# Last stage of a fused layer kernel: inputs loaded during the stage before, and one of its products issued ahead

## The reference

```python
x = layer_norm(ALPHA * x + m, lp['ln1_g'], lp['ln1_b'])            # h below
x = layer_norm(ALPHA * x + grouped_moe(x, router_w, router_b, lp['e_w1'], lp['e_w3'], lp['e_w2']),
               lp['ln2_g'], lp['ln2_b'])
...
def layer_norm(x, g, b):
    mu = xf.mean(-1, keepdims=True)
    var = jnp.square(xf - mu).mean(-1, keepdims=True)
    return ((xf - mu) * lax.rsqrt(var + LN_EPS) * g + b)
...
gate = gate / gate.sum(-1, keepdims=True)     # two experts for each frame, in grouped_moe
out = out.at[tok_pad].add(y_pad * gate_pad)   # each frame: the sum of its two gated expert rows
```

## Time and profile before

| what | value |
|---|---|
| median of 3 runs | 3728.18 us (3726.44 to 3731.19) |
| profiled execution, its own time | 3730.97 us |
| its span in the trace | 3728.8 us |
| last record of PE in `experts` starts | 3609.45 us |
| `combine` starts (its first transfer is issued) | 3614.01 us |
| `combine`, to the end of the span | 114.8 us |

### The profile page before, as it was taken

How to read it: one execution, slowest core, us unless ns; L and a number is a source line. 1 busy time by engine, 2 the same in 40 slices (tenths; PEclk the granted TensorE clock), 3 DMA queues, 4 the chain that set the end, 5 groups by cost and what they waited for, 6 DMA issues and landing times. The chain is left out here.

```text
span 3728.8 us, 77062 instructions
## 1 busy us (share of the span) xinstructions
PE 3563.9 (96%) x30285; PEld 2173.9 (58%) x30286; DVE 1623.6 (44%) x3569; ACT 965.2 (26%) x1799; POOL 230.0 (6%) x350
## 2 busy tenths in 40 slices
PE   9999979999999999979999999969999999999988
PEld 5555559989898988845555655543333333333333
DVE  1222226676767777657777435541111111111118
ACT  3333322323232333235555401110000000000003
POOL 0000010000000000011100000000000000000005
PEclk9999989999999999979999999979999999999999
DMA  6222230000000000021011522236667576643437
GB/s 229 78 89 86 70 86 8 15 15 19 11 19 11 19 11 19 7 87 50 17 52 58 187 99 96 87 155 259 247 236 279 208 282 266 256 184 136 165 120 300
DMA packets 146576, 430.57 MB, mean 115 GB/s; under 512 B 30712, under 2 KB 78976, under 8 KB 134016
## 3 DMA queue, kind: packets, MB, share of 16 engines
q1 hardware_dynamic: 127776, 359.27, 26.2%
q0 software_dynamic: 11616, 42.21, 3.2%
q10 hardware_dynamic: 6912, 25.17, 1.8%
HBM read 750.99 MB, written 78.27 MB: 222 GB/s over the span
## 5 line engine op out<-in xcount | busy, mean ns | idle before, releaser
L791 PE MATMUL rp_pa<-r_xT,w_rwkv 128*128 128x128 f32 x3808 | 480.4, 281 | 10.9 <-DMA r_xT<-scratch_xT 10.9
L307 PE MATMUL fp<-f_w,f_xT 128*128 128x411 f32 (+1 forms) x1360 | 483.0, 511 | 2.2 <-ACT f_xT L374 2.2
L791 PEld LDWEIGHTS rp_pa<-r_xT,w_rwkv 128*128 128x128 f32 x3808 | 446.6, 193 | 37.8 <-issue 26.7
L307 PEld LDWEIGHTS fp<-f_w,f_xT 128*128 128x128 f32 x1360 | 253.4, 190 | 199.3 <-issue 196.4
L2934 PE MATMUL e_H<-rows_in,e_xT 128*64 128x512 f32 x768 | 347.1, 606 | 19.1 <-DMA rows_in<-in_moe_w 17.4
L2935 PE MATMUL e_H<-fy,e_xT 128*64 x768 | 346.9, 606 | 0.0
L2953 PE MATMUL e_Y<-e_w,e_gT 128*64 128x512 f32 x768 | 339.8, 595 | 1.0 <-DMA e_w<-in_moe_w 1.0
L2935 PE MATMUL e_H<-e_w,e_xT 128*64 x768 | 339.8, 595 | 0.0
L2954 PE MATMUL e_Y<-e_w,e_gT 128*64 x768 | 339.8, 595 | 0.0
L2934 PE MATMUL e_H<-shared,e_xT 128*64 128x512 f32 x768 | 339.8, 595 | 0.0
L2934 PEld LDWEIGHTS e_H<-rows_in,e_xT 128*64 128x64 f32 x768 | 107.0, 140 | 239.0 <-issue 215.0
(11 more groups left out here) (440 smaller groups left out, 5590.9 us busy)
## 6 DMA issues: line engine op xcount, KB each, us to landing
e_w<-in_moe_w SPq DMA_DIRECT2D x144, 2048.0 KB
fy<-in_moe_w SPq DMA_DIRECT2D x48, 2048.0 KB
rows_in<-in_moe_w SPq DMA_DIRECT2D x48, 2048.0 KB
shared<-in_moe_w SPq DMA_DIRECT2D x48, 2048.0 KB
scratch_ypad<-e_y ACTq DMA_DIRECT2D x48, 512.0 KB, 2.7
scratch_xT<-f_xT SPq DMA_DIRECT2D x17, 512.0 KB, 5.3
r_xT<-scratch_xT SPq DMA_DIRECT2D x17, 512.0 KB, 3.8
scratch_h<-m_h SPq DMA_DIRECT2D x17, 512.0 KB, 2.6
```

Of the source, the lines that this page charges most:

```text
L307: mm = eng.matmul(A[n][:, 0:width], xT[:, t % 2, k, :], w[:, k, CUTS[n]:CUTS[n + 1]], start=(k == 0), stop=(k == KD - 1))
L791: mm = eng.matmul(pre_bank(bank)[:, f * P:(f + 1) * P], w[:, d, (i + f) * P:(i + f + 1) * P], xT[:, slot, d, :], start=(d == 0), stop=(d = ...
```

## The change

- After its last weight load in `experts`, SP issues the loads of all 17 tiles' frames and of the two parameter rows, 19 transfers of 512 KB, into `shared[0]` (tiles 0 to 3), `fy` (4 to 11), `rows_in` slot 1 (12, 13), `e_x` (14, 15) and `shared[1]` (16); `gain` and `offset` go to `rows_in` slot 0. In front of the parameter rows there is a wait for "h1" of block 47, in front of the last load one for "h3" of block 47.
- `combine` lies inside the scope that holds these places, and has no frame loads of its own. On SP only the 17 stores are left.
- PE makes the frame products of both halves of a tile together. Those of tiles 0 to 3 come first; that of tile t + 2 comes behind the y products of tile t, from t = 2 on.

```diff
--- before.py
+++ after.py
@@ -2889,6 +2889,20 @@
             body(BLOCKS - 2, 0)
             body(BLOCKS - 1, 1, last=True)
 
+
+            def frames(t):
+                sp.dma_start(keep["z_h"][t], io["h"][t * P:(t + 1) * P, :]).then_inc(keep["z_h_loaded"][t % 4], 16)
+
+            for t in range(4):
+                frames(t)
+            sp.wait_ge(*pe.after("h1", BLOCKS - 1))
+            sp.dma_start(keep["z_gain"], io["ln2_g"].broadcast_to([P, D])).then_inc(keep["z_weights_loaded"], 16)
+            sp.dma_start(keep["z_offset"], io["ln2_b"].broadcast_to([P, D])).then_inc(keep["z_weights_loaded"], 16)
+            for t in range(4, NT):
+                frames(t)
+            sp.wait_ge(*pe.after("h3", BLOCKS - 1))
+            frames(NT)
+
         @block.gpsimd
         def _(eng):
             pool.begin(eng)
@@ -3063,16 +3077,15 @@
 
         SLOTS = 4
         Z = [ctx.enter_context(nc.psum_tensor(f"z_Z{s}", [P, D], F32)) for s in range(SLOTS)]
-        gain, offset = sb("z_gain", [P, D]), sb("z_offset", [P, D])
-        h = sb("z_h", [P, SLOTS, D])
+        gain, offset, h = keep["z_gain"], keep["z_offset"], keep["z_h"]
         y = sb("z_y", [P, SLOTS, 2, D])
         scaled = sb("z_scaled", [P, P])
         diag = sb("z_diag", [P, SLOTS, 2, P])
         z = sb("z_z", [P, SLOTS, D])
         stats, mv, std = sb("z_stats", [P, SLOTS, 2, 6]), sb("z_mv", [P, SLOTS, 5]), sb("z_std", [P, SLOTS])
-        weights_loaded = sem("z_weights_loaded")
+        weights_loaded = keep["z_weights_loaded"]
         scaled_made = sem("z_scaled_made")
-        h_loaded = [sem(f"z_h_loaded{s}") for s in range(SLOTS)]
+        h_loaded = keep["z_h_loaded"]
         y_loaded = [sem(f"z_y_loaded{s}") for s in range(SLOTS)]
         stored = [sem(f"z_stored{s}") for s in range(SLOTS)]
         pe = Steps(sem("z_pe_steps"), ["sum"])
@@ -3089,12 +3102,6 @@
 
         @block.sync
         def _(sp):
-            def load(t):
-                s, _ = turn(t)
-                if t >= SLOTS:
-                    sp.wait_ge(*pe.after("sum", t - SLOTS))
-                sp.dma_start(h[:, s, :], io["h"][t * P:(t + 1) * P, :]).then_inc(h_loaded[s], 16)
-
             def store(t):
                 s, _ = turn(t)
                 sp.wait_ge(*pool.after("out", t))
@@ -3102,15 +3109,7 @@
                 dst = io["y_sample"][0] if t == NT else io["y_prompt"][0, t * P:(t + 1) * P, :]
                 sp.dma_start(dst, z[0:NEW if t == NT else P, s, :]).then_inc(stored[s], 16)
 
-            load(0)
-            load(1)
-            sp.dma_start(gain[:, :], io["ln2_g"].broadcast_to([P, D])).then_inc(weights_loaded, 16)
-            sp.dma_start(offset[:, :], io["ln2_b"].broadcast_to([P, D])).then_inc(weights_loaded, 16)
-            load(2)
-            load(3)
             for t in range(TILES):
-                if t + SLOTS < TILES:
-                    load(t + SLOTS)
                 store(t)
             for s in range(SLOTS):
                 sp.wait_ge(stored[s], 16 * len(range(s, TILES, SLOTS)))
@@ -3143,20 +3142,33 @@
         def _(eng):
             pe.begin(eng)
             eng.wait_ge(scaled_made, 1)
-            for t in range(TILES):
+
+            def frame(t):
                 s, n = turn(t)
-                eng.wait_ge(h_loaded[s], 16 * (n + 1))
+                eng.wait_ge(h_loaded[s], 16 * len(range(s, TILES, SLOTS)))
                 if t >= SLOTS:
                     eng.wait_ge(*act.after("norm", t - SLOTS))
                 for half in (0, 1):
                     at = slice(half * HALF, (half + 1) * HALF)
-                    eng.matmul(Z[s][:, at], scaled[:, :], h[:, s, at], start=True, stop=False)
-                    if half == 0:
-                        eng.wait_ge(*diags.after("diag", t))
-                        eng.wait_ge(y_loaded[s], 32 * (n + 1))
+                    eng.matmul(Z[s][:, at], scaled[:, :], h[t][:, at], start=True, stop=False)
+
+            def experts_rows(t):
+                s, n = turn(t)
+                eng.wait_ge(*diags.after("diag", t))
+                eng.wait_ge(y_loaded[s], 32 * (n + 1))
+                for half in (0, 1):
+                    at = slice(half * HALF, (half + 1) * HALF)
                     for i in (0, 1):
                         mm = eng.matmul(Z[s][:, at], diag[:, s, i, :], y[:, s, i, at], start=False, stop=(i == 1))
                 mm.then_inc(*pe.done("sum"))
+
+
+            for t in range(SLOTS):
+                frame(t)
+            for t in range(TILES):
+                experts_rows(t)
+                if SLOTS <= t + 2 < TILES:
+                    frame(t + 2)
 
         @block.scalar
         def _(eng):
@@ -3264,9 +3276,18 @@
                                       for n in ("w1", "w3", "w2")}
             keep["e_second_loaded"] = {n: inner.enter_context(nc.semaphore(f"e_{n}_second_loaded"))
                                        for n in ("w1", "w3", "w2")}
+
+            spots = [keep["shared"][0][:, t, :] for t in range(4)]
+            spots += [keep["fy"][:, 2 * t:2 * t + 2, :].rearrange("p a b -> p (a b)") for t in range(NT // 2)]
+            spots += [keep["rows_in"][:, 1, 0:D], keep["rows_in"][:, 1, D:2 * D]]
+            spots += [keep["e_x"][:, 0, :], keep["e_x"][:, 1, :], keep["shared"][1][:, 0, :]]
+            keep["z_h"] = spots
+            keep["z_gain"], keep["z_offset"] = keep["rows_in"][:, 0, 0:D], keep["rows_in"][:, 0, D:2 * D]
+            keep["z_weights_loaded"] = inner.enter_context(nc.semaphore("z_weights_loaded"))
+            keep["z_h_loaded"] = [inner.enter_context(nc.semaphore(f"z_h_loaded{p}")) for p in range(4)]
             mix(nc, io, keep)
             experts(nc, io, keep)
-        combine(nc, io, keep)
+            combine(nc, io, keep)
 
 
 # ---- launch: one core; inputs and outputs as the reference has them ----
```

## The result

| | before | changed |
|---|---|---|
| median (8 runs each) | 3730.36 us | 3748.83 us |
| range | 3726.44 to 3735.42 | 3741.37 to 3752.99 |
| ratio | | 1.0046 (95% interval 1.0036 to 1.0055) |
| span of the profiled execution | 3728.8 us | 3748.2 us |

By the ratio the change makes the kernel slower by 17 us (0.46%); the two medians lie 18.5 us apart. Forecast were 3725.4 us and a range from 3720.0 to 3730.5.

The account below looks back on a forecast made before the run. PE and the DMA engines (404 GB/s) were taken as the limit in the steady part. Tile 1's rows put the last statistics at 3713.9 against 3716.68, 2.8 us less: 3728.18 - 2.8 = 3725.4 us, range 3720.0 to 3730.5.

Parts of the forecast that it names:

- PE's 16 records start at 3619.9: Start of `combine`: PE begins the leading frame products of tiles 0 to 3 then, through at 3629.0, before tile 0's rows.
- rival (c): Start of `combine`: SP held until nearly the whole queue has moved, start from 3624 on; +6.7 us, 3734.9; chance 0.08.
- Y0: In `combine`, landing of tile 0's gathered rows, forecast 3631.1; from it the last statistics start at 3713.1 or later.
- Y1: In `combine`, landing of tile 1's gathered rows, forecast 3635.3; its bound on the last statistics, 3713.9, was the latest.
- Y2: In `combine`, landing of tile 2's gathered rows, forecast 3637.9; its bound on the last statistics was 3713.1.
- Rival (a): Start of `combine`: SP does not stall, ACT's store sets a start of 3615.2 to 3617; -4.2 to -2.4 us; chance 0.25.
- SP held by its queue: End of `experts`: about 1250 packets fit, 8.7 of 19 loads, so SP's last issue ends at 3618.9.
- ACT's last store: End of `experts`: sharing with q1, 2.6 us of data and some 1.5 us more before the first packet; landing 3615 to 3617.
- Shares of the gathers: In `combine`: gathers on q0 and loads on q1 share the DMA engines half and half, 2.6 us per tile's two gathers.
- PE's clock: Start of `combine`: 5 slow and 11 fast records make the 16 early ones take 9.1 us.
- rival (d): Start of `combine`: clock falls again between tile 0's and tile 1's rows, 1.3 us past tile 1's; -1.5 us, 3726.7; within forecast's 0.55.
- The step at the end: End of `combine`: tile 16's statistics come 4.76 us after tile 15's, DVE's floor; 1.33 us given back; steady step 5.15 us.

Follow-up runs that it names:

- e1: The changed kernel, but PE's frame product of a tile waits for that tile's own load, not the slot's full count; 3735.45 us, ratio 1.0005.
- e5: As e2, but the other 11 frame loads are all issued at once at the start of `combine`; 3733.48 us, ratio 1.0006.
- e2: As e1, but only 8 of the 19 transfers early, tile t + 6's load issued in `combine` after tile t's sum; 3727.00 us, ratio 0.9986.
- e7: The changed kernel, full counts kept, with SP's 19 transfers issued ahead of its last weight load instead of behind it; 3723.42 us, ratio 0.9985.
- e3: The kernel before with PE's new order alone; loads stay in `combine`, each frame product waits for its own load; 3740.60 us, ratio 1.0023.
- e8: As e7, but with PE's order of the kernel before; 3726.59 us, ratio 0.9993.
- e6: As e2, but only frames 0 to 3 and the parameter rows early, frames 4 and 5 at the start of `combine`; 3726.39 us, ratio 0.9986.
- e4: As e1, but with PE's order of the kernel before; 3733.14 us, ratio 0.9999.

## Why the prediction was wrong

**The step that failed** is the sentence "PE's 16 records start at 3619.9", 0.5 us after the forecast start of `combine`, with no term for the wait in front of them. They started at 3644.02, 22.1 us after the start of `combine`. I took the waits of the leading frame products as each tile's own, as before. The diff changes the count in the same line, and the rows of PE's order name only the semaphore, not its value. e1 is the test: with each tile's own count the wait is gone, and 15.2 us of D. With the full count the start is the landing of the last load. My own terms give its time: the 19 loads (25.3 us), ACT's stores (2.6) and eight gathers (10.4) from 3604.6 make 3642.9, +40.2; it was +38.4. With three measured figures, 10.1 us for PE's 16 records, 78.4 us from the first statistics to the last and the tail of 12.1 us, and 3.4 us for tile 0's rows, the first statistics stand at +53.7 (measured +52.2) and D is 144. Had I read the count, the sum would have come out some 18 us slower than before. No rival had this mechanism; rival (c) had the nearest shape, a start held until the queue is empty, and ended at +6.7.

**A slip in the sum.** Without the full count the kernel would still not have been 2.8 us faster: e1 has 1.3 us more in D than before. The forecast gives q1 6.8 us of work when the gathers begin. Shared half and half, it moves 2.6 of them in the 5.2 us up to Y0's last data, which leaves 4.2; the sum goes on with 1.6, as though q1 had had the engines to itself. With 4.2, Y1 is 3636.3 and Y2 3640.5 (+33.6 and +37.8), Y2's bound is the latest, 3715.7, and the gain is 1.0 us, not 2.8. Rival (a), worked out with the right halves, has no such slip. In e1 the rows landed at +32.1 and +38.2. So of the 3.0 us by which the third was late, 2.6 are the slip. It and the 1.7 us of the clock in e1's gaps make up most of the 4.1 us between the forecast and e1.

Point by point:

- **SP held by its queue:** right. Forecast for the last issue's end +16.2, measured +15.6; the later issues 1.0 us and more. It was weighed against the Trainium skill, "DMA: Bandwidth & Descriptors", section "Anatomy of one DMA — SWDGE (gpsimd) path", by which a lot of descriptors go out before their cost shows up. The section is on gpsimd's path; carried over to SP's queue it would have given +9.0, and this trace doesn't bear that out. While the store lands as late as it does, SP's being held costs nothing (e5).
- **ACT's last store:** the mechanism was right, the size wrong. Forecast +12.3 to +14.3 for its landing, measured +15.9. The half share was right: 2.7 us from the first packet to the last. The "some 1.5 us more before the first packet" had no row behind it, and it was 3.6 us more (4.4 against 0.8). The trace of before had such a case, which I left out: the store issued at 2762.0, behind weight loads on q1, took 10.2 us. The start of `combine`, forecast +16.7 by SP's last issue, was +16.4. That it came so near is in part luck, for the late store alone gives the same start (e2, e5).
- **Shares of the gathers:** right. In e1 q0 and q1 stand at 50.7% and 51.7% while both have work; the sum then applied the halves wrongly, as said above. A second, smaller thing was not in it: in the changed kernel the 5 us around the store moved 339 GB/s, not 404.
- **PE's clock:** 9.2 to 9.8 us for the 16 early records in e1, e2 and e7 (forecast 9.1); 10.1 us in the changed kernel. The clock fell again in e1's gaps, which rival (d) had at 1.3 us; it cost 1.7.
- **The step at the end:** right. In the changed kernel the last two statistics are 4.65 us apart (forecast 4.76), and the steady part is 5.15 us a tile. The 4.6 us given back come from three places. The first step is 3.36 us, since two tiles' rows lie behind each other, where it was 5.07. The next four are 4.65, 4.63, 4.63 and 4.97 us, near DVE's own floor, where they were 5.15. At the end the last step saves 0.5 us, and the kernel before had one step of 5.87 us. The DMA share in the steady part was 0.90 to 0.96, not near 75%.
- **The order costs nothing by itself:** wrong without early loads (e3: 8.6 us), right with them.

## What to carry to other kernels

Read the count of a wait, not only its semaphore: a total in place of a running number turns "this tile" into "all of them". Ask of a transfer that is moved ahead what it will then stand in front of: here a store that all engines wait for, and the gathers. The place for it is where the queue and the DMA engines were idle: the same 19 loads, issued 18.7 us earlier, turned a loss of 17 us into a gain of 5.6 (by the ratios). A new order of products needs its inputs ahead of it, and is to be judged together with them.

## What was not expected of the hardware

A store of 512 KB on ACT's queue took 2.7 us to land with nothing on SP's queue. It took 3.8 to 4.2 us where 111 to 212 packets of SP's queue moved between its issue and its last packet and were then all gone (e7, e8, e6; a load has 144), and 7.1 to 8.2 us where 480 or more did (e5, e2, e1, the changed kernel, e4). Half shares account for 1.3 us more. The rest is a wait ahead of the store's first packet: 0.8 us after the issue in e7, e8 and before, 1.4 in e6, 4.0 to 4.4 in the other five, while 362 to 393 packets of SP's queue went by. What holds the store back is open. SP's own stall doesn't, since in e2 and e5 SP issues nothing in that time.
